# Where a kernel of 17 stages clears its semaphores: in blocks of their own, or inside the next stage

## The chip, the cores and the metric

The kernel runs on one core of a Trainium2 chip. The metric is the device time of one execution in microseconds (us); it is given as the median of several runs. A profiled execution of the same program gives the trace that the rows below are taken from. Of the core's engines, TensorE (PE) multiplies matrices, VectorE (DVE), ScalarE (ACT) and GpSimd (POOL) do the elementwise work, and SyncE (SP) has no arithmetic: it issues transfers and handles semaphores.

## The reference

Two decoder layers over a sequence of 1024 tokens of width 1024, in float32.

```python
for i in range(DEPTH):                      # DEPTH = 2
    a = _rms_norm(h, norm_mix[i])
    h = h + (_even_mixer(a, ...) if i % 2 == 0 else _odd_mixer(a, ...))
    h = h + _hier_moe(_rms_norm(h, norm_ffn[i]), ...)
    h = h + _per_layer_embedding(h, p[i], ...)
```

The even mixer is causal attention with 8 forgetting heads and 8 latent heads; the odd one is a diagonal state-space layer (S5) beside a gated DeltaNet in chunks. The mixture of experts sends each token to 2 of 32 experts (a group first, then two of its eight). The per-layer embedding is a sigmoid gate times a small projection. None of this is touched by the change.

## The kernel before, in words

The program is a straight row of 17 stages; nothing of one stage runs beside another. In order, with the number of semaphores each uses: the constants (2), the even layer's projections (51), its attention (23), the end of the mixer with output projection and routing (37), the experts' first blocks (20), the overflow blocks (12), the layer embedding (26); then for the odd layer the norm (12), a joint stage of S5 columns and powers (14), the S5 chunks (18), a joint stage of the S5 gate, masks, gates and DeltaNet inputs (29), the DeltaNet's preparation (40) and scan (13), the end of the mixer (37), first blocks (20), overflow blocks (12) and the layer embedding (26). Together 392.

A stage is one `nc.Block()`: a region in which every engine gets its own instruction stream, and at whose end all five engines meet at a barrier. [...] Inside a block the engines are tied by semaphores that count up from zero, for transfers (16 each) and for instructions (1 each). The counts in the waits are constants of the stage, so a semaphore must be zero again before its number is given to another stage.

The helper `stage` (line 83) allocates a stage's semaphores, opens the block (line 93) and, when that is closed, calls `clear` (lines 74 to 79 and 95). `clear` opens a second block (line 75) in which SyncE alone has instructions: one `sem_clear` per semaphore (line 79). The other four engines go straight to that block's barrier. Only behind it does the next stage begin. `joint_stage` (line 56) does the same for several helpers that share a block (line 58); their semaphores are gathered in `joint.sems` and cleared at line 61.

```python
def clear(nc, sems):
    with nc.Block() as clearing:
        @clearing.sync
        def _(sp):
            for s in sems:
                sp.sem_clear(s)
```

In the trace the barrier that closes a stage stands under line 93 (15 stages) or 58 (2 joint stages), and the barrier of the clearing block under line 75.

What SyncE does in the stages that matter here: in `overflow_blocks` (line 1530) every engine loads a count of blocks that did not fit and goes through a loop only if it is above zero; with these inputs it is zero. In `layer_embedding` (line 1874) SyncE issues six loads, then for each of 8 token tiles waits until the tile is added and issues its store (line 1919), and at the end waits until all 8 stores have landed. In the norm in front of the odd layer (`rmsnorm_transpose`, line 136) it issues two loads and waits for the second. In the experts' first blocks (line 1623) it issues the weights' loads into a ring of eight places (line 1674). At the start of attention (line 266) TensorE turns queries and keys through one bank (line 362), which ACT and DVE empty in turn. The end of the mixer begins with the output projection on TensorE (line 1243).

Of the kernel before, what the change touches and what calls it, by code (L numbers as in the profile page):

```python
# [30 lines left out]
NUMBER = itertools.count()  # L31


class Steps:
# [3 lines left out]
    def __init__(self, eng, sem, base=0):  # L38
        self.eng, self.sem, self.base, self.n = eng, sem, base, 0
# [7 lines left out]
class Joint:  # L47

    def __init__(self, block, memory):
        self.block, self.memory, self.sems = block, memory, []


@contextmanager
def joint_stage(nc):
    with ExitStack() as memory:
        with nc.Block() as block:
            joint = Joint(block, memory)
            yield joint  # L60
        clear(nc, joint.sems)


@contextmanager
def scope(joint=None):

    if joint is not None:
        yield joint.memory
    else:
        with ExitStack() as memory:  # L70
            yield memory


def clear(nc, sems):
    with nc.Block() as clearing:  # L75
        @clearing.sync
        def _(sp):
            for s in sems:
                sp.sem_clear(s)


@contextmanager
def stage(nc, *names, joint=None):

    with scope(joint) as ctx:
        sems = [ctx.enter_context(nc.semaphore(f"{n}_{next(NUMBER)}")) for n in names]
        if joint is not None:
            joint.sems += sems  # L90
            yield joint.block, sems
            return
        with nc.Block() as block:
            yield block, sems
        clear(nc, sems)


def sbuf(nc, ctx, name, shape, dt=F32):

    return ctx.enter_context(nc.sbuf_tensor(f"{name}_{next(NUMBER)}", shape, dt))  # L100
# [11 lines left out]
def make_constants(nc, c):  # L112

    with stage(nc, "zeroed", "selected") as (block, (zeroed, selected)):
        @block.gpsimd
        def _(pool):
            pool.memset(c.ident[:], 0.0).then_inc(zeroed, 1)
            pool.memset(c.ones[:], 1.0).then_inc(zeroed, 1)
            pool.memset(c.causal[:], 0.0).then_inc(zeroed, 1)
            pool.wait_ge(zeroed, 3)  # L120
            pool.affine_select(out=c.ident[:], in_=c.ident[:], compare_op=ALU.not_equal, fill=1.0,
                               base=0, pattern=[[-1, P]], channel_multiplier=1).then_inc(selected, 1)

            pool.affine_select(out=c.upto[:], in_=c.ones[:], compare_op=ALU.is_ge, fill=0.0,
                               base=0, pattern=[[1, P]], channel_multiplier=-1).then_inc(selected, 1)
            pool.affine_select(out=c.before[:], in_=c.ones[:], compare_op=ALU.is_gt, fill=0.0,
                               base=0, pattern=[[1, P]], channel_multiplier=-1).then_inc(selected, 1)

            pool.affine_select(out=c.causal[:], in_=c.causal[:], compare_op=ALU.is_ge, fill=NEG,
                               base=0, pattern=[[-1, P]], channel_multiplier=1).then_inc(selected, 1)  # L130
            pool.wait_ge(selected, 4)
            pool.tensor_copy(c.ident16[:], c.ident[:])
            pool.tensor_copy(c.causal16[:], c.causal[:])


def rmsnorm_transpose(nc, c, h, gain, normed, xt, width=D, x_dram=None, loads=(), joint=None, h_ready=None):
# [4 lines left out]
    with scope(joint) as ctx:  # L141
# [4 lines left out]
        rstd = sbuf(nc, ctx, "rstd", [P, NT])  # L146
        turned = [psum(nc, ctx, f"turned{a}", [P, 2 * SLAB]) for a in range(2)]
        with stage(nc, "h0_in", "h1_in", "gain_in", "loaded", "squares", "means", "roots", "scaled", "turns", "copied_even",
                   "copied_odd", "vec_steps", joint=joint) as (block, (h0_in, h1_in, gain_in, loaded, squares, means, roots, scaled, turns,
                                                          copied_even, copied_odd, vs)):  # L150
# [115 lines left out]
def attention(nc, c, both, heads, pt, dv, loads):  # L266
# [21 lines left out]
    with ExitStack() as ctx:  # L288
# [10 lines left out]
        turn_high = psum(nc, ctx, "turn_high", [P, SLAB])  # L299
        po = psum(nc, ctx, "po", [2 * dv, SLAB])  # L300
        with stage(nc, "qk_turned", "qk_act", "qk_dve", "scored", "maxed", "exped", "low0_turned", "low1_turned",
                   "high0_turned", "high1_turned", "low0_out", "low1_out", "high0_out", "high1_out", "mixed", "mixed_out",
                   "inverse_turned", "inverted", "inverse_spread", "stored", "loaded", "zeroed", "zeros_out") as (
# [788 lines left out]
def constants(nc, ctx):  # L1092
    c = Constants()
    c.ident, c.ones, c.upto, c.before, c.causal = [
        sbuf(nc, ctx, n, [P, P]) for n in ("ident", "ones", "upto", "before", "causal")]

    c.ident16, c.causal16 = [sbuf(nc, ctx, n, [P, P], BF16) for n in ("ident16", "causal16")]


    c.slots_in = nc.dram_tensor("slots_in", (EXPERTS * REGION + P, D), F32).ap()  # L1100
    c.slots_out = nc.dram_tensor("slots_out", ((2 * EXPERTS + NT) * P, D), F32).ap()
    c.scattered = ctx.enter_context(nc.semaphore("scattered"))
    c.rows_in = [ctx.enter_context(nc.semaphore(f"rows_in{n}")) for n in range(4)]
    c.x_in = [ctx.enter_context(nc.semaphore(f"x_in{n}")) for n in range(2)]
    c.y_out = [ctx.enter_context(nc.semaphore(f"y_out{n}")) for n in range(2)]
    c.h_kept = nc.dram_tensor("h_kept", (S, D), F32).ap()
    make_constants(nc, c)
    return c
# [741 lines left out]
def routing(nc, ctx):  # L1850
    r = Routing()
    r.weights = sbuf(nc, ctx, "weights", [P, 2, NT])
    r.slots, r.results = [sbuf(nc, ctx, n, [P, 2, NT], I32) for n in ("slots", "results")]
    r.table = sbuf(nc, ctx, "table", [1, 5, EXPERTS + 1], I32)
    return r
# [1267 lines left out]
def odd_mixer(nc, c, t, h, layer, r):  # L3123
# [4 lines left out]
    with ExitStack() as ctx:  # L3128
# [9 lines left out]
        with ExitStack() as sub:  # L3138
            q = s5_tiles(nc, sub, h)
            bpow = sbuf(nc, sub, "bpow", [P, 2, PAIRS, P])  # L3140
            with joint_stage(nc) as joint:
                products, evacuate = s5_columns(nc, c, xt, w_in, gbz, u, early, slab_place(h[:, 0:4]), joint)
                s5_powers(nc, c, t, j, q, bpow, joint, products, evacuate)
            s5_chunks(nc, c, t, j, q, bpow, u, scratch=s5_t)
# [5 lines left out]
        with ExitStack() as heads:  # L3150
# [6 lines left out]
            with ExitStack() as prepare:  # L3157
                k = Masks()
                gdn_mask_places(nc, k, prepare)
                with joint_stage(nc) as joint:  # L3160
                    gdn_masks(nc, c, k, joint)
                    sig = sbuf(nc, joint.memory, "sig", [P, 2, SLAB])
                    s5_glu(nc, c, t, j, output_of(u), work[:, 8:12], sig, s5_t, joint)
                    load_rows(nc, [(gains[:], t["gdn_o_norm"][j])], joint)
                    sums, sums_out = gdn_gates(nc, c, t, j, gbz, g, joint)
                    delta_inputs(nc, c, xt, w_in[:, OD_QKV:OD_G], t["gdn_conv_w"][j], [slab_place(work[:, 0:4]), slab_place(work[:, 4:8])],
                                 sig[:].rearrange("p a n -> p (a n)").rearrange("p (t d) -> p t d", t=NT), qkv, sums, sums_out, joint)
                gdn_prepare(nc, c, g, k, qkv, wt, qt, intra_t, scratch)
# [24 lines left out]
def trunk(nc, t, out):  # L3193


    with ExitStack() as ctx:
        c = constants(nc, ctx)
        h = sbuf(nc, ctx, "h", [P, NT, D])
        r = routing(nc, ctx)
        even_mixer(nc, c, t, h, 0, r)  # L3200
        layer_embedding(nc, c, t, h, 0, r, out_dram=c.h_kept)
        odd_mixer(nc, c, t, h, 1, r)
        layer_embedding(nc, c, t, h, 1, r, out_dram=out[0])


# [16 lines left out]
```

## Time and profile before

| What | us |
|---|---|
| Median of 3 runs | 3204.94 (3203.44 to 3205.21) |
| The profiled execution's own time | 3205.38 |
| Its span, from first to last record | 3203.8 |
| TensorE busy | 2941.1 (92%) |
| VectorE busy | 1127.8 (35%) |
| ScalarE busy | 652.4 (20%) |
| GpSimd busy | 242.8 (8%) |
| Mean granted TensorE clock | 0.949 of full |
| DMA, all queues | 617.24 MB, 193 GB/s over the span |

The span is what the trace covers; 1.6 us of the device time lie around it. Register, branch, semaphore and drain instructions are not counted as busy, so a stretch in which all engines only meet at barriers shows as idle on every one of them. "SPq", "PEldq" and the like are the sequencers' own instructions on that engine. [...]

### The profile page before, as it was taken

The page shows a single profiled execution, that of the slowest core. Times are in us where ns is not written, and L with a number is a line of the kernel's source. Part 1 is how long each engine was busy: PE and PEld are TensorE (multiplying, and loading weights), DVE is VectorE, ACT ScalarE, POOL GpSimd, SP SyncE. Part 2 cuts the span into 40 slices and gives each one's busy share as a digit, 9 for nine tenths or more (in the row PEclk, how much of TensorE's full clock was granted, in tenths as well). Part 3 has the DMA queues.
Part 4 walks back from the last instruction along what each step waited for, and adds up shares of the span by engine and source line. Part 5 has one row for each costly group of instructions (what it writes and reads, how often), then busy time and mean ns, then how long its engine had stood idle before and what let it go on. Part 6 is the DMA issues. An engine that isn't in the chain of part 4 may idle for free. (4 is left out here: it accounts for less than half of the span.)

```text
span 3203.8 us, 32783 instructions
## 1 busy us (share of the span) xinstructions
PE 2941.1 (92%) x12473; PEld 1581.4 (49%) x12474; DVE 1127.8 (35%) x2460; ACT 652.4 (20%) x1258; POOL 242.8 (8%) x352
## 2 busy tenths in 40 slices
PE   7999899999799999979889899877997999999798
PEld 5544555545444444424376644476654444444243
DVE  2584355534300000005273625466463000000052
ACT  3310355521110010103121123322211100101030
POOL 0000000001100000011000000043211000000110
PEclk9999899999799999989988799988997999999899
DMA  4000791031599999963120110000415999999641
GB/s 155 27 27 0 309 373 53 1 114 66 198 421 414 413 403 401 400 237 155 44 66 1 15 67 27 0 2 2 167 66 190 422 413 411 410 404 397 233 162 40
DMA packets 138550, 617.24 MB, mean 193 GB/s; under 512 B 25188, under 2 KB 31748, under 8 KB 121992
## 3 DMA queue, kind: packets, MB, share of 16 engines
q1 hardware_dynamic: 110952, 525.93, 41.6%
q0 software_dynamic: 24064, 86.00, 7.0%
q10 hardware_dynamic: 3376, 3.19, 0.3%
q8 instruction: 101, 1.65, 0.2%
q14 instruction: 57, 0.47, 0.0%
HBM read 508.00 MB, written 105.91 MB: 192 GB/s over the span
## 5 line engine op out<-in xcount | busy, mean ns | idle before, releaser
L1974 PE MATMUL acc<-wg,xt 128*128 128x512 f32 x512 | 223.1, 599 | 0.0
L2570 PE MATMUL acc<-xt,work 128*128 128x512 f32 x384 | 166.9, 593 | 0.0
L737 PE MATMUL acc<-h,xt 128*128 128x512 f32 x384 | 165.2, 592 | 0.0
L1974 PEld LDWEIGHTS acc<-wg,xt 128*128 128x128 f32 x512 | 98.5, 193 | 123.4 <-issue 123.4
L376 PE MATMUL scores<-qkt 65*128 65x512 f32 (+7 forms) x384 | 148.9, 498 | 0.9 <-DVE qkt L516 0.9
L522 DVE TENSOR_REDUCE nmax<-scores 128x1 f32<-128x256 f32 (+7 forms) x128 | 96.8, 756 | 77.6 <-PE scores L378 74.5
L1720 PE MATMUL py<-place 128*64 128x512 f32 (+1 forms) x352 | 120.2, 594 | 1.0 <-DVE place L1800 1.0
L1720 PE MATMUL pu<-place 128*128 128x512 f32 (+1 forms) x320 | 119.8, 593 | 0.0
L737 PEld LDWEIGHTS acc<-h,xt 128*128 128x128 f32 x384 | 72.9, 190 | 91.1 <-issue 90.9
L1243 PE MATMUL acc<-place 128*128 128x512 f32 x256 | 114.2, 601 | 2.7 <-PEq L75 2.7
L2570 PEld LDWEIGHTS acc<-xt,work 128*128 128x128 f32 x384 | 72.0, 190 | 86.1 <-issue 86.1
L1806 DVE COPY work<-py 128x512 f32<-128x512 f32 x25 | 17.3, 691 | 242.8 <-PE py L1720 242.8
L1806 DVE COPY place<-py 128x512 f32<-128x512 f32 x25 | 17.3, 691 | 241.1 <-PE py L1720 241.1
L1720 PE MATMUL pg<-place 128*128 128x512 f32 (+1 forms) x288 | 101.6, 596 | 0.0
L469 ACT ACTIVATE probs<-scores,nmax 128x256 f32<-128x256 f32 (+7 forms) x128 | 94.3, 736 | 9.0 <-DVE nmax L522 7.6
L833 ACT ACTIVATE place<-acc 128x256 f32<-128x256 f32 (+4 forms) x88 | 39.8, 473 | 243.3 <-PE acc L737 243.2
L2247 PE MATMUL acc<-s_t,xt 128*128 128x260 f32 (+1 forms) x256 | 86.5, 501 | 2.5 <-PEq L75 2.5
L1839 DVE TENSOR_TENSOR place<-place,pu 128x512 f32<-128x512 f32 x25 | 17.2, 688 | 187.3 <-PE pu L1720 187.3
L1839 DVE TENSOR_TENSOR work<-work,pu 128x512 f32<-128x512 f32 x25 | 17.2, 687 | 186.2 <-PE pu L1720 186.2
L1787 ACT ACTIVATE place<-pg 128x512 f32<-128x512 f32 x25 | 14.9, 597 | 329.1 <-PE pg L1720 329.1
L1787 ACT ACTIVATE work<-pg 128x512 f32<-128x512 f32 x25 | 14.9, 597 | 328.0 <-PE pg L1720 328.0
L376 PEld LDWEIGHTS scores<-qkt 65*128 65x128 f32 (+1 forms) x384 | 64.2, 194 | 33.8 <-issue 33.4
(638 smaller groups left out, 5181.0 us busy)
## 6 DMA issues: line engine op xcount, KB each, us to landing
own<-in_moe_w_gate_dram SPq DMA_DIRECT2D x22, 2048.0 KB, 16.1
place<-in_moe_w_down_dram SPq DMA_DIRECT2D x22, 2048.0 KB, 15.8
place<-in_moe_w_up_dram SPq DMA_DIRECT2D x20, 2048.0 KB, 17.4
slots_out<-zeros SPq DMA_DIRECT2D x4, 9216.0 KB, 62.6
place<-in_moe_w_gate_dram SPq DMA_DIRECT2D x18, 2048.0 KB, 20.5
own<-in_moe_w_up_dram SPq DMA_DIRECT2D x16, 2048.0 KB, 15.4
own<-in_moe_w_down_dram SPq DMA_DIRECT2D x10, 2048.0 KB, 18.9
xt<-in_moe_w_gate_dram SPq DMA_DIRECT2D x9, 2048.0 KB, 22.2
```

The lines of the kernel that those rows point to most:

```text
L376: pe.matmul(bank(n, u)[:, a * SLAB:a * SLAB + w], qkt[0:kind(p).rows, p % 2, u, 0, i * P:(i + 1) * P], qkt[0:kind(p).rows, p % 2, u, 1, a ...
L469: act.activation(probs[:, u, n % 2, 0:(i + 1) * P], bank(n, u), ACT.Exp, bias=nmax[:, n % 2, u:u + 1], accum_out=total[:, (n // NT) % 2, i ...
L522: dve.tensor_reduce(nmax[:, n % 2, u:u + 1], bank(n, u), AX.X, ALU.max, negate=True).then_inc(maxed, 1)
L737: last = pe.matmul(acc[:, n % 4, 0:width], xs[:, k, tile_of(i)], weights[:, k, cols], start=(k == 0), stop=(k == k_of - 1))
L833: last = act.activation(place, part, ACT.Copy)
L1243: last = pe.matmul(acc[:, n, :], columns(k, i), slabs[n][:, k, :], start=(k == 0), stop=(k == KD - 1))
L1720: last = pe.matmul(out[part], lhs[:, k, part], weights_of(kind, q)[:, k, cols], start=(k == 0), stop=(k == k_last), skip_group_check=True)
L1806: dve.tensor_copy(y[:, n % 2, SLAB:D], py[:, SLAB:D]).then_inc(y_dve, 1)
L1839: dve.tensor_tensor(hid, gate, pu[:], ALU.mult).then_inc(hidden, 1)
L1974: last = pe.matmul(acc[:, u % 4, :], xt[:, k, i * P:(i + 1) * P], wg[:, k, n * SLAB:(n + 1) * SLAB], start=(k == 0), stop=(k == KD - 1))
L2247: ins = pe.matmul(acc[:, n % 4, 0:width], xt[:, k, at], slab[:, k, 0:width], start=(k == 0), stop=(k == KD - 1))
L2570: last = pe.matmul(acc[:, n % 4, :], slabs[m // 4 % 2][:, k, (m % 4) * P:(m % 4 + 1) * P], xt[:, k, half * SLAB:(half + 1) * SLAB], start= ...
```

## The change

The clears of a stage move into the next stage's block. A block is now opened by `one_block`, which gives SyncE one more body behind all it has in this block; that body clears the semaphores of the stage before (`Used.sems`). The semaphores stay allocated until then: `Used.held` is closed when the next block is. After the last stage `clear_last` clears that stage's semaphores in a block of its own, as before. The stages' own instructions are the same.

```diff
@@ -47,18 +47,50 @@
 class Joint:
-    def __init__(self, block, memory):
-        self.block, self.memory, self.sems = block, memory, []
+    def __init__(self, block, memory, held):
+        self.block, self.memory, self.held, self.sems = block, memory, held, []
+
+class Used:
+    sems, held = [], None
+
+@contextmanager
+def one_block(nc, held, sems):
+    with nc.Block() as block:
+        yield block
+        if Used.sems:
+            @block.sync
+            def _(sp):
+                for s in Used.sems:
+                    sp.sem_clear(s)
+    if Used.held is not None:
+        Used.held.close()
+    Used.sems, Used.held = sems, held
+
+def clear_last(nc):
+    with nc.Block() as clearing:
+        @clearing.sync
+        def _(sp):
+            for s in Used.sems:
+                sp.sem_clear(s)
+    Used.held.close()
+    Used.sems, Used.held = [], None
 
 @contextmanager
 def joint_stage(nc):
+    held, sems = ExitStack(), []
     with ExitStack() as memory:
-        with nc.Block() as block:
-            joint = Joint(block, memory)
+        with one_block(nc, held, sems) as block:
+            joint = Joint(block, memory, held)
+            joint.sems = sems
             yield joint
-        clear(nc, joint.sems)
@@ -71,28 +103,16 @@
-def clear(nc, sems):
-    with nc.Block() as clearing:
-        @clearing.sync
-        def _(sp):
-            for s in sems:
-                sp.sem_clear(s)
 
 @contextmanager
 def stage(nc, *names, joint=None):
-    with scope(joint) as ctx:
-        sems = [ctx.enter_context(nc.semaphore(f"{n}_{next(NUMBER)}")) for n in names]
-        if joint is not None:
-            joint.sems += sems
-            yield joint.block, sems
-            return
-        with nc.Block() as block:
-            yield block, sems
-        clear(nc, sems)
+    held = ExitStack() if joint is None else joint.held
+    sems = [held.enter_context(nc.semaphore(f"{n}_{next(NUMBER)}")) for n in names]
+    if joint is not None:
+        joint.sems += sems
+        yield joint.block, sems
+        return
+    with one_block(nc, held, sems) as block:
+        yield block, sems
@@ -3201,6 +3221,7 @@
         layer_embedding(nc, c, t, h, 1, r, out_dram=out[0])
+        clear_last(nc)
```

## Rows read from the trace of the kernel before

**Rows 1.** The page, busy us (share of the span) and instructions of TensorE.
```profile
PE 2941.1 (92%) x12473; PEld 1581.4 (49%) x12474; DVE 1127.8 (35%) x2460; ACT 652.4 (20%) x1258; POOL 242.8 (8%) x352
```

**Rows 2.** Windows, one per clearing block: start:end us, busy us per engine, PEclk, DMA, GB/s.
```profile
3.55:3.92 0.37, 0.00 (x0) 0.00 (x0) 0.00 (x0) 0.00 (x0) 0.00 (x0) 1.00 0.00 0
333.96:337.72 3.76, 0.00 (x0) 0.00 (x0) 0.00 (x0) 0.00 (x0) 0.00 (x0) 0.75 0.00 0
682.66:684.22 1.56, 0.00 (x0) 0.00 (x0) 0.00 (x0) 0.00 (x0) 0.00 (x0) 0.92 0.00 0
...
3030.75:3031.67 0.92, 0.00 (x0) 0.00 (x0) 0.00 (x0) 0.00 (x0) 0.00 (x0) 0.50 0.09 18
sum 25.76, PE 0.00 PEld 0.00 DVE 0.00 ACT 0.00 POOL 0.00; mean PE 0.00 PEld 0.00 DVE 0.00 ACT 0.00 POOL 0.00
```

**Rows 3.** Line 79: whole span; windows 333:338, 1590:1599.5, 2240.8:2241.3. ns min/median/max, first to last start us.
```profile
L79 SPq EVENT_SEMAPHORE_RANGE_CLEAR  x392: 25/30/49, 3.7 to 3203.5; - x196
...
L79 SPq EVENT_SEMAPHORE_RANGE_CLEAR  x51: 25/30/38, 334.1 to 337.0; - x51
...
L79 SPq EVENT_SEMAPHORE_RANGE_CLEAR  x26: 25/28/30, 1597.8 to 1599.2; - x26
...
L79 SPq EVENT_SEMAPHORE_RANGE_CLEAR  x2: 31/31/31, 2240.8 to 2241.3; - x2
```

**Rows 4.** Waits of SyncE's queue: waited for, us in total, times, longest.
```profile
SPq L93 <- PEq L93: 876.6, 15, 163.2
...
SPq L58 <- PEq L58: 235.2, 2, 127.1
```

**Rows 5.** Line 93, window 1599.4:1622.95, the norm in front of the odd layer.
```profile
L93 SPq DRAIN  x1: 7/7/7, 1607.2 to 1607.2; - x1
...
L93 DVEq DRAIN  x1: 1258/1258/1258, 1621.5 to 1621.5; - x1
```

**Rows 6.** Line 93, window 1425:1427.4, the first overflow block.
```profile
L93 SPq DRAIN  x1: 7/7/7, 1426.6 to 1426.6; - x1
...
L93 PEldq DRAIN  x1: 72/72/72, 1427.2 to 1427.2; - x1
```

**Rows 7.** Line 93, window 3027:3031.7, the second overflow block.
```profile
L93 SPq DRAIN  x1: 7/7/7, 3030.2 to 3030.2; - x1
...
L93 PEldq DRAIN  x1: 71/71/71, 3030.6 to 3030.6; - x1
```

**Rows 8.** Line 93, windows 1590:1599.5 and 3201:3204, the ends of the layer embeddings.
```profile
L93 DVEq DRAIN  x1: 725/725/725, 1594.1 to 1594.1; - x1
...
L93 SPq DRAIN  x1: 7/7/7, 1597.6 to 1597.6; - x1
...
L93 SPq DRAIN  x1: 7/7/7, 3201.4 to 3201.4; - x1
```

**Rows 9.** Windows around the start of mixer's end, of attention, and in the S5 chunks.
```profile
681.76:684.35 2.59, 0.00 (x0) 0.00 (x1) 0.69 (x1) 0.00 (x0) 0.00 (x0) 0.93 0.00 0
684.40:687.40 3.00, 3.00 (x4) 1.45 (x5) 2.53 (x69) 0.00 (x0) 0.53 (x5) 0.50 0.57 193
...
333.26:337.85 4.59, 0.00 (x0) 0.00 (x0) 0.00 (x0) 0.55 (x1) 0.01 (x1) 0.78 0.00 0
337.85:352.70 14.85, 8.90 (x32) 5.75 (x33) 2.75 (x4) 3.65 (x5) 0.94 (x1) 0.50 0.89 356
352.70:363.10 10.40, 10.37 (x38) 7.94 (x39) 3.85 (x9) 3.84 (x13) 0.00 (x0) 0.50 1.02 407
...
1742.10:1783.00 40.90, 40.75 (x184) 26.25 (x185) 6.85 (x12) 7.16 (x12) 0.00 (x0) 0.50 0.07 7
```

**Rows 10.** Timeline behind the first clearing block: start us, us, engine, what.
```profile
4.04 0.39 SPq L715 DMA_DIRECT2D h<-in_x_dram  x1
...
4.12 0.07 DVE L978 MEMSET prefix<- 128x8 f32 x1 [4.01 <-PEq L75]
```

**Rows 11.** The page, DMA queues: packets, MB, share of 16 engines.
```profile
q8 instruction: 101, 1.65, 0.2%
```

## The prediction

> **What bounds the kernel now.** I first read the busy shares on the page [rows 1]: TensorE works for 2941.1 of 3203.8 us, so the kernel is a row of stages that TensorE fills, and what is left is at most 8% of the span. The change touches only the seams between stages, so the next view is the windows one, cut at the seams. A seam begins when the barrier that closes a stage's block is released (events of line 93, or 58 for a joint stage) and ends when the barrier of the clearing block (line 75) is released. In [rows 2] each such stretch has zero busy time on all five engines and next to no DMA (0.09 at most); the 16 seams that the change removes last 25.76 us together, from 0.37 to 3.76 us each. The reader is to see the zeros: nothing is hidden there, so whatever a seam gives back, the whole program behind it gets. No transfer spans a seam that could become a wait once the seam is shorter.
>
> Then the clears themselves [rows 3]: 392 of them, all by SyncE, one after another. 51 fit between 334.1 and 337.0, which is 2.9 / 50 = 0.058 us from one to the next; 26 between 1597.8 and 1599.2 give 0.056. I use 0.057. What remains of the shortest seam is 0.37 - 2 x 0.057 = 0.26 us: the barrier alone.
>
> Last, where SyncE stands when a block ends. The waits of SyncE's own queue [rows 4] show it waiting 876.6 us in all at the 15 closing barriers of line 93 and 235.2 us at the two of line 58: in most stages it has long finished.
>
> **What the change removes.** 16 of the 17 clearing blocks (the last one stays, as `clear_last`, with the same 26 clears): 16 x 0.26 = 4.2 us of barriers, 366 x 0.057 = 20.9 us of clears, together 25.1; measured 25.76, because in a few seams SyncE stalls between two clears, as at 2240.8, where the next comes at 2241.3 [rows 3]. The term is the measured one: **-25.8 us**.
>
> **What it moves.** The clears go behind SyncE's own program of the next block, so they cost nothing where SyncE is early by more than their length, and all where it is last. No instruction is queued behind them but the block's drain. Block by block:
> - Twelve of the 16 following blocks have cover from the work of the other engines. The tightest is the norm in front of the odd layer: SyncE drains at 1607.2, DVE's drain of 1258 ns starts at 1621.5 [rows 5], so 26 clears (26 x 0.057 = 1.5 us) have 15 us of room. Cost 0. Were that cover gone, all 366 would cost 20.9 us and only the 4.2 us of barriers would be won (a rival below).
> - The first overflow block has no work (its count is zero), so no engine is long in it. SyncE drains at 1426.6, TensorE last at 1427.2 for 72 ns [rows 6]. 20 clears of the block before take 1.14 us: SyncE is now there at 1426.6 + 1.14 = 1427.8, about **+0.5 us**. The second one: 3030.2 + 1.14 = 3031.3 against 3030.6 + 0.07 [rows 7]: **+0.7 us**.
> - The layer embeddings, twice. SyncE is last there: it sends the output and waits for its landing, and drains at 1597.6 when DVE has been done since 1594.1 + 0.7, and at 3201.4 in the second [rows 8]. The 12 clears of the overflow block come behind that wait: 12 x 0.057 = 0.7 each, **+1.4 us**.
> - Semaphores are held one stage longer, so numbers differ; the sum of neighbouring stages is small (51 + 23 the largest), nothing is issued for that. Cost 0.
>
> **The clock of TensorE.** At 682 the clock is full until the seam, TensorE then sits for 2.59 us without work, and the next 3.00 us run at 0.50 with TensorE busy throughout (four matmuls of 512 columns) [rows 9]. The seam itself is 1.56 us, so the idle stretch shrinks to 1.0 us. Half of 3.0 us, **-1.5 us**, would come back if the shorter gap keeps the clock; if not, 0. I take the gain, since work at full density stands on both sides. At the start of attention the clock is low for 25 us after a gap of 4.59 us [rows 9], but the work there is thin (TensorE busy 8.90 of 14.85 us): I take 0 and keep the bound for a rival.
>
> **Costs that no row shows.** With the seam goes the time in which the engines' sequencers could fetch what comes next. Bounds: below 0, by the seam of 0.37 us, after which SyncE and DVE start the next stage's first instructions at 4.04 and 4.12, 0.12 and 0.20 us behind the release at 3.92 [rows 10]. That start needs no more than a barrier's worth of idle time. Above, one stall of the size seen among the clears (0.5 less the pace, 0.43 us) at each of 16 seams, 6.9 us. I take 0, by the nearer row, and keep 6.9 for the range.
>
> [...]
>
> **Sum** against the profiled execution (span 3203.8, time 3205.4, so 1.6 lies around the span): 3203.8 - 25.8 + 0.5 + 0.7 + 1.4 - 1.5 = 3179.1; plus 1.6 = 3180.7. The median of the three runs, 3204.94, is 0.4 below the profiled one, so **3180.3 us**, 0.77% less.
>
> **Rivals.**
> - *The clock stays up through the seams.* Attention's head would run at full speed: TensorE's busy time from 337.85 to 363.1 is 8.90 + 10.37 = 19.3 us at 0.50 [rows 9], so at most 9.6 us more are won: 3180.3 - 9.6 = 3170.7. For it: the 4.59 us gap falls to 0.8. Against: from 1742.1 on, TensorE is busy 40.75 of 40.90 us and stays at 0.50 [rows 9]; narrow matmuls and transposes are slow there for ten times as long as any gap lasts. Chance 0.12. [...]
> - *Exposed fetches, partly.* The page counts 101 packets of the queue q8 "instruction" with 0.2% of 16 engines' span [rows 11]: 0.002 x 3203.8 x 16 / 101 = about 1.0 us each. Anything from 0.43 to 1.0 us at each seam costs 6.9 to 16 us: 3187 to 3196, still faster. Chance 0.12.
> - *SyncE is late everywhere*, or the barriers stay: the clears move without cover and only barriers are won: 3204.9 - 4.2 = 3200.7, within 0.2%. Against it stand the 1112 us that SyncE waits [rows 4]. Chance 0.04.
> - *Slower: fetches on the path at each seam.* [...] Price: more than one packet of 1.0 us in sequence per seam. The net gain of 23.2 us is used up at 23.2 / 16 = 1.45 us per seam, and it is slower by 0.2% beyond 1.85; two packets each give 3204.9 - 23.2 + 32 = 3213.7. Rows 10 speak against it. Chance 0.02.
>
> **How the numbers follow.** Forecast as summed 0.70, clock rival 0.12, partly exposed fetches 0.12, no gain 0.04, slower 0.02. A measurement of this kernel tells about 0.2% (6.4 us) from no change. The first three are all faster by more: 0.94; within 0.2%: 0.04; slower: 0.02. Range: low 3171, the clock rival in full; high 3189, the forecast with 6.9 us of stalls and without the clock's 1.5. What falls outside is part of the fetch rival and the last two, some 0.15.
>
> **What would show it.** In the profile after, right: one clearing block instead of 17, at the end, still some 2.2 us; 16 barriers fewer; the first instruction of each stage 0.1 to 0.2 us behind the release of the block before; 392 clears in all, 366 of them while other engines are busy; SyncE last at the barrier in both overflow blocks and in both layer embeddings, with the 12 clears between its last wait and its drain; full clock from the first matmul behind attention. Each stage's own length otherwise the same: a stage that grew by over 1 us at its start speaks for the fetch rival, one that shrank by some us for the clock. The forecast is wrong if SyncE's drain comes last in a block not named here, or if the time is not between 3171 and 3189.

## The result, and the profile after

The changed kernel takes **3159.26 us** (median of four runs: 3159.78, 3158.57, 3158.73, 3178.30) against 3204.63 for the kernel before on the same chip: ratio 0.9873, 95% interval 0.9836 to 0.991. The forecast was 3180.3 with a range of 3171 to 3189. The sign was right, but the gain is 45.4 us where 24.6 were forecast, and the time lies below the range. The profiled execution took 3159.78 us over a span of 3158.2, against 3205.38 and 3203.8 before: 45.6 us less.

The page of the changed kernel, busy us per engine, beside [rows 1]:

```profile
PE 2916.5 (92%) x12473; PEld 1569.3 (50%) x12474; DVE 1128.2 (36%) x2460; ACT 652.6 (21%) x1258; POOL 243.5 (8%) x352
```

This is the first sign of what happened. The same 12473 matmuls are busy 24.6 us less, while the busy times of VectorE, ScalarE and GpSimd stand within 0.7 us of where they were. The 16 seams that went have 0.00 us of busy time on every engine [rows 2], so their removal does not explain this. A higher granted clock does: its mean went from 0.949 to 0.959, and 18.9 of the 24.6 us lie in one stage, the S5 chunks, where TensorE's busy time for the same 544 matmuls fell from 97.94 to 79.06 us while the granted clock rose from 0.70 to 0.86 (windows below).

The parts that the prediction named, first. Lines of clears, SyncE's waits and SyncE's drains in the changed kernel (70 is the line of the clears in the next block, 81 that of the last block, 64 the barrier that closes a stage). The windows are the whole span for the first three, then the closing of the first overflow block, of the second, and of the last layer embedding:

```profile
L70 SPq EVENT_SEMAPHORE_RANGE_CLEAR  x366: 25/30/39, 222.8 to 3156.2; - x183
L81 SPq EVENT_SEMAPHORE_RANGE_CLEAR  x26: 25/28/30, 3156.5 to 3157.9; - x26
...
SPq L64 <- PEq L64: 1089.1, 17, 164.3
...
L70 SPq EVENT_SEMAPHORE_RANGE_CLEAR  x20: 25/30/31, 1410.6 to 1411.7; - x20
...
L64 PEldq DRAIN  x1: 71/71/71, 1410.8 to 1410.8; - x1
...
L64 SPq DRAIN  x1: 7/7/7, 1411.8 to 1411.8; - x1
...
L64 PEldq DRAIN  x1: 69/69/69, 2984.2 to 2984.2; - x1
...
L64 SPq DRAIN  x1: 7/7/7, 2985.4 to 2985.4; - x1
...
L64 SPq DRAIN  x1: 7/7/7, 3156.3 to 3156.3; - x1
```

All 366 clears are there, and SyncE still waits 1089.1 us at the 17 closing barriers. In both overflow blocks its drain now comes about 1 us behind TensorE's, as its 20 clears lie there. The last block is still there, with 26 clears.

The start of the second stage, behind the release at 3.55, in the timeline of the changed kernel:

```profile
3.67 0.39 SPq L735 DMA_DIRECT2D h<-in_x_dram  x1
...
3.74 0.07 DVE L998 MEMSET prefix<- 128x8 f32 x1 [3.63 <-PEq L64]
```

0.12 and 0.19 us behind the release, as in [rows 10]. In each of the 16 stages some engine has its first instruction 0.10 to 0.13 us behind the release: no delay at a stage's start speaks for the rival of exposed fetches.

Now each stage's own length, from the release of one closing barrier to the next. The release is told by GpSimd's second semaphore event at the barrier. At the first clearing block of the kernel before that event is at 3.9 us, behind the drains of all five engines (3.6 to 3.8) and ahead of one event on each of the other four (4.0):

```profile
L75 POOLq EVENT_SEMAPHORE  x2: 17/17/17, 3.8 to 3.9; - x2
L75 POOLq DRAIN  x1: 41/41/41, 3.6 to 3.6; - x1
...
L75 SPq DRAIN  x1: 7/7/7, 3.8 to 3.8; - x1
L75 SPq EVENT_SEMAPHORE  x1: 17/17/17, 4.0 to 4.0; - x1
```

The lengths:

| Stretch | Before | After | Difference |
|---|---|---|---|
| 16 seams | 25.76 | none | -25.8 |
| projections | 330.03 | 329.47 | -0.6 |
| attention | 344.94 | 340.08 | **-4.9** |
| end of the even mixer | 163.06 | 161.60 | -1.5 |
| first overflow block | 1.67 | 2.58 | +0.9 |
| first layer embedding | 169.38 | 171.11 | +1.7 |
| S5 columns and powers (joint) | 116.95 | 118.37 | +1.4 |
| S5 chunks | 111.57 | 92.94 | **-18.6** |
| DeltaNet's preparation | 163.31 | 166.03 | +2.7 |
| scan | 34.97 | 33.66 | -1.3 |
| end of the odd mixer, first blocks | 746.26 | 744.64 | -1.6 |
| second overflow block | 1.46 | 2.58 | +1.1 |
| second layer embedding | 169.88 | 170.91 | +1.0 |
| last clearing block | 2.18 | 1.71 | -0.5 |

The other four stretches differ by 0.2 us in sum. The seams gave what was forecast. One stage that the prediction took to stay as it was gave 18.6 us more. Windows of the S5 chunks, in the kernel before (the first 30 us, then the stage; the figure behind the five engines is PEclk, the granted clock as a share of full):

```profile
1741.81:1771.81 30.00, 29.84 (x132) 18.73 (x133) 4.91 (x11) 4.18 (x7) 0.00 (x0) 0.51 0.01 1
1741.81:1853.37 111.56, 97.94 (x544) 71.26 (x544) 57.69 (x94) 15.39 (x25) 0.00 (x0) 0.70 0.10 11
```

and in the changed one (the first 30 us, the stage, then the stage cut where the clock changes):

```profile
1724.94:1754.94 30.00, 27.56 (x256) 21.49 (x256) 13.36 (x25) 10.30 (x17) 0.00 (x0) 1.00 0.22 23
1724.94:1817.88 92.94, 79.06 (x544) 61.51 (x544) 57.71 (x94) 15.18 (x25) 0.00 (x0) 0.86 0.13 14
...
1725.10:1757.80 32.70, 27.56 (x256) 21.46 (x256) 16.19 (x29) 10.40 (x17) 0.00 (x0) 1.00 0.27 29
1757.80:1764.60 6.80, 3.63 (x33) 3.33 (x33) 6.65 (x13) 0.00 (x0) 0.00 (x0) 0.50 0.39 41
1764.60:1798.70 34.10, 30.92 (x202) 23.77 (x200) 30.98 (x49) 3.58 (x6) 0.00 (x0) 1.00 0.00 1
```

The stage has 544 matmuls in both. Before, it runs its first 132 in 30 us at a clock of 0.51. After, it runs 256 in 30 us at 1.00, and TensorE even has gaps (27.56 of 30 us busy). The stretch of [rows 9] that was low for 41 us is gone. What stays low is what was low before as well: 6.8 us at 1757.8 (then at 1793.3), in a wait of TensorE for VectorE (TensorE busy 3.63 us of them, VectorE 6.65), and the last 19 us of the stage, the third line below. TensorE's idle time ahead of the stage's first matmul fell from 1.97 us to 0.94: the seam of 1.03 us was all that went. Here are that first matmul before and after, and that last stretch:

```profile
1741.97 0.96 PE L2343 MATMUL pa<-ident,bpow 128*128 128x128 f32 x4 [1.97 <-PEq L75]
...
1725.10 0.63 PE L2363 MATMUL pa<-ident,bpow 128*128 128x128 f32 x4 [0.94 <-PEq L64]
...
1798.82:1817.88 19.06, 16.96 (x56) 12.92 (x56) 3.77 (x6) 1.20 (x2) 0.00 (x0) 0.50 0.00 0
```

The gap does not leave the clock low at once. Before the change, too, the stage begins at full clock, and the clock falls 0.3 us in:

```profile
1741.81:1742.11 0.30, 0.14 (x2) 0.17 (x3) 0.11 (x4) 0.00 (x0) 0.00 (x0) 1.00 0.00 0
1742.11:1771.81 29.70, 29.70 (x132) 18.56 (x132) 4.80 (x9) 4.18 (x7) 0.00 (x0) 0.50 0.01 1
```

The two seams that the prediction looked at for their clock, in the changed kernel: the gap ahead of the mixer's end and the first matmuls behind it, then the gap ahead of attention and the stretches behind it:

```profile
672.37:673.24 0.87, 0.00 (x0) 0.02 (x1) 0.56 (x1) 0.00 (x0) 0.00 (x0) 1.00 0.00 0
673.30:676.30 3.00, 3.00 (x7) 1.36 (x8) 2.54 (x70) 0.00 (x0) 0.53 (x5) 1.00 0.59 188
...
332.30:333.20 0.90, 0.02 (x1) 0.05 (x1) 0.00 (x0) 0.57 (x1) 0.06 (x1) 1.00 0.00 0
333.17:341.20 8.03, 3.88 (x24) 2.44 (x24) 1.87 (x3) 1.78 (x3) 0.92 (x1) 1.00 0.78 314
341.20:351.50 10.30, 8.50 (x32) 6.55 (x33) 3.19 (x8) 4.40 (x12) 0.00 (x0) 0.50 1.02 408
```

At the mixer's end the clock stays at 1.00: seven matmuls start in the 3.00 us that held four in [rows 9]. Attention starts at 1.00 as well and falls 8 us in, for 10.2 us instead of 27.3.

### The profile page after: what moved, and what is told of

It reads as the page before. It is cut to its first block and busy times, and to the rows that moved or that the text cites. A ratio compares the mean times of both kernels' runs of the same rounds, so it can differ in the third digit from the quotient of the medians.

```text
span 3158.2 us, 32607 instructions
## 1 busy us (share of the span) xinstructions
PE 2916.5 (92%) x12473; PEld 1569.3 (50%) x12474; DVE 1128.2 (36%) x2460; ACT 652.6 (21%) x1258; POOL 243.5 (8%) x352
## 5 line engine op out<-in xcount | busy, mean ns | idle before, releaser
L1807 ACT ACTIVATE place<-pg 128x512 f32<-128x512 f32 x25 | 14.9, 597 | 329.0 <-PE pg L1740 329.0
L1807 ACT ACTIVATE work<-pg 128x512 f32<-128x512 f32 x25 | 14.9, 597 | 328.9 <-PE pg L1740 328.9
## 6 DMA issues: line engine op xcount, KB each, us to landing
place<-in_moe_w_up_dram SPq DMA_DIRECT2D x20, 2048.0 KB, 17.8
```

## Experiments

Two theories for the 18.6 us of the S5 chunks. **Gap**: the 1.97 us without work for TensorE ahead of this stage bring the clock down at the stage's start, and the stage's first work does not bring it back. **Place**: something else in the changed kernel (a later or earlier start, other semaphore numbers, the clears beside the work) decides. Most kernels below are the changed one with a switch: a clearing block stays behind chosen stages, with all of its clears, with none, or with small matmuls for TensorE. In all of them a stage's semaphores are given free one stage later, as in the changed kernel. "Stage 8" is the joint stage ahead of the S5 chunks, "stage 1" the projections ahead of attention.

```diff
     Used.n += 1
+    if n in KEEP:                       # clears kept in the seam block
+        with nc.Block() as clearing:
+            ... SyncE: the first KEEP[n] clears of stage n
+            ... if n in FILL: TensorE: FILL[n] times
+                pe.matmul(bank, c.ones[:], c.ident[:], ...)
```

**1. Only the S5 seam removed.** `KEEP` = every stage but 8.

> The clearing block behind the joint stage of S5 columns and powers is the only one taken away (its 14 clears move into the S5 chunks); the other 15 stay. [...] Rival 'place': the clock there depends on when the stage comes, moved by the 17 us won ahead of it, not on its own seam; then 3204.6 - 1.0 = 3203.6 us with the chunks at 111.6 us.

By the gap theory this one seam is worth 1.0 + 18.6 us: 3204.6 - 19.6 = 3185.0 us, with the chunks near 93 us.

Measured: 3183.77 us (four runs, 3182.34 to 3187.35), ratio 0.9934 (0.9917 to 0.9951). First 30 us of the chunks, and the stage:

```profile
1742.90:1772.90 30.00, 27.56 (x256) 21.50 (x256) 13.36 (x25) 10.29 (x17) 0.00 (x0) 1.00 0.22 23
1742.90:1834.22 91.32, 77.45 (x544) 60.39 (x544) 57.69 (x94) 15.18 (x25) 0.00 (x0) 0.88 0.13 14
```

One seam of 1.03 us is worth some 20 us. The gap theory stands, and the stage begins at 1742.9, 1.1 us from where it began before: the place in time is not it.

**2. Only the S5 seam kept.** `KEEP` = {8: all}.

> As after the change, but the S5 chunks' own seam (14 clears, 1.0 us) is put back. Gap: the clock is lost there again, 3159.3 + 1.0 + 18.6 = 3178.9 us, chunks near 111.6 us. Place: 3159.3 + 1.0 = 3160.3 us, chunks near 93 us.

Measured: 3176.35 us (3174.91 to 3176.55), ratio 0.9911 (0.9895 to 0.9928).

```profile
1728.68:1758.68 30.00, 29.84 (x136) 19.23 (x137) 4.90 (x11) 4.18 (x7) 0.00 (x0) 0.52 0.01 1
1728.68:1837.01 108.33, 94.72 (x544) 69.53 (x544) 57.69 (x94) 15.29 (x25) 0.00 (x0) 0.73 0.11 12
```

The slow head is back, in the otherwise changed kernel. Here the clock falls a little later, after 1.2 us of the stage; its first microsecond is still full:

```profile
1728.68:1729.68 1.00, 0.84 (x7) 0.67 (x8) 0.15 (x4) 0.17 (x1) 0.00 (x0) 1.00 0.00 0
```

Together, 1 and 2 put the effect in this seam.

**3. The S5 seam kept, TensorE busy in it.** `KEEP` = {8: all}, `FILL` = {8: 3}; the seam lasts 1.20 us.

> As the kernel with only the S5 seam kept, but TensorE runs three small float32 matmuls (12 instructions of 128 columns, some 1.3 us) of constants into a spare bank inside that clearing block; nobody reads them. [...] If the barrier or the SyncE clears themselves cost the clock, as if only the seam were kept: 3179 us. [...]

By either theory the chunks take about 93 us and the whole about 3161 us: by the gap theory because TensorE is not idle in the seam, by the place theory because the seam does not matter.

Measured: 3170.18 us (3172.83, 3155.62, 3169.89, 3170.47), ratio 0.9878 (0.9853 to 0.9903). The last line is a stretch later in the same stage:

```profile
1728.73:1758.73 30.00, 27.57 (x256) 21.52 (x256) 13.36 (x25) 10.28 (x17) 0.00 (x0) 1.00 0.22 23
1728.73:1830.82 102.09, 88.31 (x544) 68.93 (x544) 57.70 (x94) 15.18 (x25) 0.00 (x0) 0.76 0.11 12
1760.60:1791.30 30.70, 24.99 (x123) 20.13 (x123) 21.06 (x37) 1.19 (x2) 0.00 (x0) 0.50 0.11 12
```

The three small matmuls are 6 instructions in the trace, busy 0.91 us, not the 12 and 1.3 us of the estimate. The head is at full clock although the barrier and the clears stand. But here the drop that comes some 32 us into the stage lasts 30.7 us where the changed kernel's lasts 6.8. So there is a second place in this stage where the clock falls, and how long it stays low varies. The profiled span is 11.9 us above the changed kernel's with the seam taken off (3171.3 - 1.2 - 3158.2); 9.2 of them are in this stage (102.09 for 92.94) and 2.2 in attention (342.26 for 340.08). That is why the time lies between 3161 us and the 3179 us expected if the barrier or the clears themselves cost the clock.

**4. The S5 seam kept, but empty** (a barrier, no clears). `KEEP` = {8: 0}; the seam lasts 0.33 us.

> As after the change, with an empty block (a barrier, no clears, 0.26 us) at the S5 seam; its 14 clears are in the chunks. TensorE's idle stretch is 1.1 to 1.2 us, between 0.9 (clock kept) and 1.9 (lost). Gap: if the stretch has to be near 1.9 us to lose the clock, 3159.6 us with the chunks at 93; if 1.2 is already too long, 3178.2 us; runs that differ among themselves by 19 us would say that it stands on the edge. Place: 3159.6 us.

Measured: 3169.1 us, ratio 0.9899 (0.9869 to 0.9929), and the four runs are 3160.40, 3177.81, 3178.20, 3160.00. The profiled one:

```profile
1726.10:1756.10 30.00, 27.56 (x256) 21.50 (x256) 13.37 (x25) 10.29 (x17) 0.00 (x0) 1.00 0.23 23
1726.10:1818.94 92.84, 78.97 (x544) 61.54 (x544) 57.71 (x94) 15.18 (x25) 0.00 (x0) 0.86 0.13 14
```

Two groups of times 18 us apart and nothing between them. The mean granted clock of the runs differs with them: 0.959 and 0.961 in the two shorter, 0.954 and 0.953 in the two longer. With 1.27 us of idle TensorE the same program keeps its clock or loses it. A median over such runs is a count of which outcome came up, not the price of a barrier.

**5. The changed kernel again**, five runs.

> The changed kernel once more, unchanged, for the spread of its times. [...] Rival 'one value': the 3178.3 us was a disturbance; all runs within 3 us of 3159.3.

If the chunks keep the clock in most executions and lose it in some, the times fall into two groups, near 3159 and near 3178 us, in the kernel before with the weights turned round.

Measured: 3159.95 us (3158.23 to 3162.54), ratio 0.9878 (0.9855 to 0.9902). With the first four runs, eight of nine lie between 3158 and 3163 and one at 3178.3, at a clock of 0.953. The kernel before has the two groups as well: of the 49 runs made of it in all, 7 lie between 3186 and 3191 (clock 0.953 to 0.955) and 42 between 3202 and 3209 (0.947 to 0.951).

**6. The exposed clears covered.** Neither overflow block clears anything: its predecessor's semaphores are carried on, and the layer embedding's SyncE clears all 32 behind its six loads, before it waits for the first tile.

```diff
+CARRY = (5, 15)                          # the overflow blocks
+                clear_now(sp)            # layer_embedding, behind the six loads
                 for i in range(NT):
                     sp.wait_ge(added, 2 * i + 2)
```

> As after the change, but no clear is exposed: the overflow blocks clear nothing (their stage before's semaphores are carried on), and the layer embeddings clear all 32 behind their six loads, ahead of the wait for the first store. Both theories of the exposed clears say: each overflow block 2.58 to 1.67 and 1.46 us, each embedding 0.7 us shorter, 0.9 + 1.1 + 0.7 + 0.7 = 3.4 us, so 3155.9 us where the chunks keep the clock (3174.9 where they don't). If the embeddings' other 1.0 us of growth was the clock, it stays or goes by chance. If the clears among running transfers cost something, no gain.

Measured: 3159.05 us (3152.28 to 3159.98), ratio 0.9873 (0.985 to 0.9896). The clears in the first layer embedding (its line 65), then the windows of the first overflow block and of that embedding, and those of the changed kernel:

```profile
L65 SPq EVENT_SEMAPHORE_RANGE_CLEAR  x32: 2/25/273, 1436.1 to 1438.5; - x32
...
1409.31:1410.99 1.68, 0.00 (x0) 0.00 (x0) 0.00 (x0) 0.00 (x0) 0.00 (x0) 0.50 0.02 5
1410.99:1582.17 171.18, 152.62 (x400) 72.59 (x400) 67.97 (x92) 36.65 (x66) 18.21 (x16) 0.94 0.30 117
```

```profile
1409.29:1411.87 2.58, 0.00 (x0) 0.00 (x0) 0.00 (x0) 0.00 (x0) 0.00 (x0) 0.50 0.05 13
1411.87:1582.98 171.11, 153.32 (x400) 72.86 (x400) 68.03 (x92) 36.88 (x66) 18.93 (x16) 0.93 0.30 117
```

The overflow blocks are back at 1.68 and 1.48 us, so their clears had cost 0.90 and 1.10. From the last store to the end of the first embedding it is 2.88 us again instead of 3.62, so the clears there had cost 0.74. Yet the embedding is no shorter. Its part ahead of the last store took 0.8 us more than in the changed kernel (171.18 - 171.11 + 0.74). The clock is not the reason: it was low for less of the embedding (mean 0.94 for 0.93). TensorE waited longer for the projection's weights, here and in the changed kernel:

```profile
1422.75 2.47 PE L1990 MATMUL acc<-wp,pt 128*128 128x512 f32 x3 [2.40 <-DMA wp<-in_ple_w_proj_dram]
...
1422.55 3.78 PE L1977 MATMUL acc<-wp,pt 128*128 128x512 f32 x4 [0.82 <-DMA wp<-in_ple_w_proj_dram]
```

In the second embedding it is 2.62 us for 0.50. The clears come 24 us behind the issue of that load, so they are not what delayed it; SyncE's issue of it took 1.43 us for 0.58 in the first embedding and 1.68 for 0.63 in the second, and why is open. By medians the 3.4 us expected came to 0.9; this profiled execution (span 3150.7) is the shortest of the five.

**7. As 6, with three small matmuls behind the last product of the joint stage** ahead of the S5 chunks, into a spare bank, so that TensorE works up to the barrier and idles for 0.30 us ahead of the chunks.

```diff
+                if last == 3 * NT:
+                    for k in range(3):
+                        pe.matmul(spare[:], c.ones[:], c.ident[:], ...)
```

> As clears_covered, and TensorE goes on with three small float32 matmuls of constants into a spare bank behind its last product of the joint stage, while ScalarE empties the last bank, so it is idle for 0.3 instead of 0.9 us ahead of the S5 chunks. Gap: every execution keeps the clock at the start of the chunks; 3155.9 us and no second heap at +18. Rival (the loss inside the chunks, 33 us behind their start, is what varies): times still spread over up to 18 us.

Measured: 3154.73 us (3150.56 to 3158.94), ratio 0.9857 (0.9833 to 0.9882); on the same chip 5.2 us under run 5. It has the lowest median of all versions. All five runs are in the shorter group, though so were eight of nine without the tail: five runs don't show that it makes the clock safe.

**8. The attention seam kept.** `KEEP` = {1: all}; the seam lasts 3.16 us.

> As after the change, but the seam ahead of attention (51 clears, 3.8 us) is put back. Gap: attention is back at its length of before, 344.9 instead of 340.1 us, so 3159.3 + 3.8 + 4.8 = 3167.9 us where the S5 chunks keep the clock (3186.5 where they don't). Place: 3163.1 us.

Measured: 3167.47 us (3165.89 to 3167.71), ratio 0.9899 (0.9872 to 0.9927). Attention, first 25 us and whole, here, then in the changed kernel:

```profile
335.92:360.92 25.00, 18.90 (x80) 13.36 (x81) 7.46 (x15) 8.44 (x21) 0.95 (x1) 0.59 0.94 376
335.92:678.84 342.92, 315.87 (x1792) 196.11 (x1792) 182.74 (x304) 173.05 (x401) 0.95 (x1) 0.97 0.43 172
```

```profile
333.02:358.02 25.00, 18.91 (x94) 13.35 (x95) 9.73 (x18) 10.36 (x26) 0.95 (x1) 0.80 0.94 376
333.02:673.09 340.07, 313.00 (x1792) 194.08 (x1792) 182.74 (x304) 173.25 (x401) 0.95 (x1) 0.98 0.44 174
```

Attention gives back 2.8 us of its 4.9; with the seam's 3.2 that is 6.0 of the 6.1 us between the two profiled spans (3164.3 and 3158.2). The median rose by 7.5 over run 5; the other 1.4 us have no place in this profile. The 2.8 us are not all the seam's: in the profiles of runs 2 and 3, which have no seam here, attention takes 342.24 and 342.26 us, with the clock falling 4.4 us in. Attention's length without a seam thus varies from 340.1 to 342.3, and one profile of each kernel does not show how much of the 4.9 us is the gap's.

**9. All seams there, TensorE busy in 15 of them** (4 to 15 small matmuls each). The seams then last 43.6 us together, 17.8 more than before.

> All 16 clearing blocks are kept as before the change, but behind 15 of them (all but the first) TensorE multiplies constants (4 to 15 small float32 matmuls, about as long as the clears take) into a bank nobody reads any more. No seam is removed, so no part of the 25.8 us is won; exposed clears (3.4 us) are not paid either. Gap: the clock's share of the gain comes alone: attention -4.9, end of the mixer -1.5, S5 chunks up to -18.6 (some executions -9, as with only that seam filled): 3203 - 6.4 - 9 to 18.6 = 3178 to 3188 us. Rival 'it is the removed time that counts, the clock follows the place': 3203 us.

Measured: 3189.51 us (seven runs, 3185.9 to 3199.18), ratio 0.9961 (0.9942 to 0.9979). The S5 chunks, and attention's first 25 us:

```profile
1742.05:1833.38 91.33, 77.45 (x544) 60.38 (x544) 57.72 (x94) 15.18 (x25) 0.00 (x0) 0.88 0.13 14
...
336.95:361.95 25.00, 18.89 (x84) 13.26 (x85) 8.37 (x16) 9.24 (x23) 0.95 (x1) 0.66 0.94 375
```

Its profiled span is 3185.9: 3203.8 + 17.8 of longer seams leaves 35.7 us that the stages gave, with no barrier and no clear removed. That is what the clock can give where TensorE works through 15 of the seams; in the changed kernel the stages gave 45.6 - 25.8 = 19.8 us. It comes from the S5 chunks (-20.2), the experts' first blocks (571.3 each, -3.4 and -4.1), attention (-3.0) and smaller ones. The first blocks were not expected to give anything.

**10. The attention seam kept, TensorE busy in it.** `KEEP` = {1: all}, `FILL` = {1: 15}; the seam lasts 3.88 us.

> As attention_seam_kept (3167.5 us, attention 342.9 us in its profile), with TensorE busy with 15 small matmuls in that seam. [...]

By the gap theory attention is back near 340.1 us and the whole at 3159.5 + 3.8 = 3163.3 us; if idling is not the reason, it stays at 3167.5.

Measured: 3165.89 us (3164.91 to 3167.21), ratio 0.9886 (0.9863 to 0.991); attention 342.23 us, hardly less than the 342.92 of run 8. **Not what was expected**: the clock falls at 340.5, 4 us into attention, whatever went before it, for 17.1 us. With the gap closed or filled, attention still loses the clock within 4 to 8 us. Its head is thin work (TensorE busy 3.88 of 8.03 us in the changed kernel's window above), which may be the reason; no run made it denser. What a gap changes is how soon the clock falls: in run 8 after 1.2 us of attention, in the kernel before already in the seam.

**11. All seams there, all empty.** `KEEP` = every stage with 0 clears; each lasts 0.33 us.

> As after the change, with an empty block (barrier, no clears) at each of the 16 seams. Gap: only 0.3 us more without work at each seam, 3159.5 + 16 x 0.3 = 3164.3 us where the S5 chunks keep the clock, some 3182 where they do not, and both heaps seen, as with the empty block at that seam alone (3160.0 and 3160.4, 3177.8 and 3178.2). If the barriers carried more of the 25.8 us than 0.26 each, it is slower than this by the difference.

Measured: 3180.16 us (3182.04, 3180.64, 3179.68, 3164.47), ratio 0.9914 (0.9885 to 0.9943); the profiled one:

```profile
1729.28:1759.28 30.00, 29.84 (x140) 19.20 (x140) 4.90 (x11) 4.18 (x7) 0.00 (x0) 0.54 0.01 1
1729.28:1839.39 110.11, 96.48 (x544) 71.16 (x544) 57.71 (x94) 15.39 (x25) 0.00 (x0) 0.71 0.11 11
```

16 barriers of 0.33 us are 5.3 us, and the short run stands just that above the changed kernel's. The other three, one of them the profiled run, stand 15 to 18 us higher. In the profiled one the first 2.00 us of the chunks still run at 1.00, then the clock falls. The barrier itself took 0.33 us, and here three runs of four were 15 to 18 us longer: it adds 0.33 us to a gap of 0.94.

**12. All seams there, TensorE busy in the S5 seam alone.** Every clearing block stands with all of its clears, as in the kernel before; four small matmuls are in the block behind stage 8. Besides them only one thing differs from the kernel before: semaphores are given free one stage later, as in runs 1 to 4.

```diff
+KEEP = {0: None, 1: None, ... 15: None}   # None: all clears of that stage
+FILL = {8: 4}
```

> All 16 clearing blocks as before the change; the one edit is 4 small float32 matmuls of constants on TensorE in the block ahead of the S5 chunks (into a bank nobody reads any more). In the kernel with all seams filled that seam took 1.43 us instead of 1.03. [...] Place: 3204.7 us, with 3187 as seldom as in the kernel before (4 of 33).

By the gap theory the chunks start at full clock in every execution: 3204.3 + 0.4 - 18.6 = 3186.1 us where they keep it to the end, some 3195 where they lose it 33 us in, and none near 3204.

Measured: 3187.55 us (11 runs, 3185.38 to 3193.16), ratio 0.9959 (0.9944 to 0.9975) against 3202.98 for the kernel before beside it.

```profile
1740.57:1770.57 30.00, 27.56 (x256) 21.48 (x256) 13.38 (x25) 10.29 (x17) 0.00 (x0) 1.00 0.22 23
1740.57:1833.99 93.42, 79.55 (x544) 61.89 (x544) 57.69 (x94) 15.18 (x25) 0.00 (x0) 0.85 0.13 13
...
1739.31 1.13 PE L93 MATMUL pc<-ident,ones 128*128 128x128 f32 x8 [0.94 <-PEq L68]
...
1740.73 0.63 PE L2389 MATMUL pa<-ident,bpow 128*128 128x128 f32 x4 [0.30 <-PEq L83]
```

The last two lines are the small matmuls and the first one of the chunks: TensorE's idle time of 1.97 us is cut into 0.94 and 0.30.

The seam became longer (1.43 us for 1.03), the kernel does more work, and it is 15.4 us faster by medians. All eleven runs are under 3194, where only 7 of 49 of the unedited kernel are. Each other stage is within 1 us of its length in the kernel before. Later release of the semaphores is not the reason, since run 2 has it and the slow head as well. This settles the cause: it is TensorE's idling at this seam.

The outcomes at the S5 seam side by side; the group of each run is told by its time and granted clock, and only one run of each kernel has a trace. Run 3 is left out, since its second drop hides the first outcome in the times:

| TensorE at the S5 seam | Idle ahead of the chunks | Clock kept, runs |
|---|---|---|
| idle, barrier and clears (kernel before; run 2) | 1.97 us | 7 of 49; 0 of 4 |
| idle, barrier alone (runs 4, 11) | 1.27 us | 2 of 4; 1 of 4 |
| no seam (changed kernel; runs 1, 6, 8, 10) | 0.94 us | 8 of 9; 17 of 17 |
| working in the seam (runs 9, 12) | 0.94 us, then 0.30 | 6 of 7, one unclear (3199.18); 10 of 11, one unclear (3193.16) |
| no seam, working up to the barrier (run 7) | 0.30 us | 5 of 5 |

## Why the prediction was wrong, step by step

**The seams, -25.8: right.** They are gone to the hundredth, since nothing was hidden in them and nothing filled them.

**Hidden clears at 0, held semaphores at 0: right.** All stages but those named have SyncE waiting at the end as before.

**The overflow blocks, +0.5 and +0.7: right in place, too small.** Measured +0.9 and +1.1, and run 6 takes them back in full. The 20 clears take the 1.1 us that they were priced at (1410.6 to 1411.7). But they were priced as starting where SyncE's drain had stood, 0.9 us into the stage (1426.6 - 1425.7), and they start 1.3 us in (1410.6 - 1409.3). Why SyncE comes to them 0.4 us later is not shown.

**The embeddings' ends, +0.7 each: right.** From the last store to the end it is 3.62 us for 2.88, and 3.65 for 2.90. The stages grew by 1.7 and 1.0 in all. The remaining 1.0 and 0.3 lie ahead of the first store. TensorE's clock fits them: it comes back up 14.8 us into the first embedding for 10.0 before, and 14.7 for 14.3 in the second. No run was made for it.

**No exposed fetch, 0: right.** First instructions come 0.12 to 0.19 us behind the release in either kernel. That anything is fetched while the engines idle in a seam was an assumption; no run shows it. The trace gives no cause for the stall of 0.43 us between two clears either, so that it was a fetch, as the fetch rival's price took it, is not shown.

**The clock at the mixer's end, -1.5: right**, 1.46 us. Run 9 bears it out: with its seam longer but filled, that stage takes 161.69 us for 163.06.

**The clock elsewhere, 0: the step that failed.** The words were that from 1742.1 on "narrow matmuls and transposes are slow there for ten times as long as any gap lasts", and they served as the reason against the rival of a clock that stays up. The row [rows 9] (40.75 of 40.90 us busy at 0.50) was read as what that work does to the clock. It was the outcome of the gap ahead of it: the same matmuls run at 1.00 for their first 30 us where the idle time ahead is 0.94 us or is filled (runs 1, 3 and 12). Half right was that this work does not bring the clock back: it stayed low for 41 us with TensorE busy throughout. The row had the warning in it. By the halving that the prediction used for attention, this work at full clock needs about half of 40.75 us, so a bound of 20 us belonged into the range beside attention's 9.6; 18.6 were measured. The two seams that I did examine were chosen for their low clock behind them, and at this third one the low clock was put down to the stage.

**The rival "the clock stays up": right in kind, wrong in its places.** It had attention's head alone, at -9.6, and a chance of 0.12. Attention gave half of that in the profiled run, where its head still loses the clock 8 us in; the S5 chunks gave twice it. The gap that decided was short: 1.97 us ahead of the chunks against 0.94.

The sum with what was measured: 3203.8 - 25.8 (seams) - 18.6 (chunks) - 4.9 (attention) - 1.5 (mixer's end) + 2.0 (overflow) + 2.8 (embeddings) + 4.1 (columns, preparation) - 3.8 (all others) = 3158.1, against a span of 3158.2. The 4.1 us of the columns and the preparation go with a clock that falls at another moment than before: in the columns 7.8 us in, behind a wait of TensorE of 3.05 us (before, low from the start for 5.6 us, with a wait of 0.61), and in the preparation for 46.8 us in all instead of 40.6. No run was made for them, so their cause is not shown.

## What to carry to other kernels

Price an idle stretch of TensorE twice: by its own length, and by the low clock behind it, which here lasted 41 us although TensorE was busy all the time; take half of the busy time at 0.50 behind each gap as the bound (20 us for the chunks, where 18.6 were won; 9.6 for attention, where 4.9 were). A row of work at low clock does not say whether the work or the gap ahead of it is the cause, so look whether the same kind of work runs at full clock elsewhere, or put a few small matmuls in the gap. When runs fall into two groups, count the groups before comparing medians.

## What the runs showed of the hardware that was not expected

- A stage with two outcomes: in the profiles the same S5 chunks take 91 to 93 us, or 108 to 112 us where the clock falls at their start (and 102 once, in run 3, by the later drop). By the times, it fell in 5 of 8 runs with a gap of 1.27 us and in 46 of 53 with 1.97.
- The clock does not fall in that gap but behind it, with TensorE at work again: 0.3, 1.2 and 2.4 us into the stage in the kernel before and runs 2 and 11. It then stays low for 40.9, 37.1 and 37.6 us, with TensorE busy in all but 0.15 us of it.
- An empty block at a seam took 0.33 us (runs 4 and 11), and runs with it at the S5 seam came out 15 to 18 us longer in 5 of 8 cases.
- With TensorE busy through the seams (run 9) the experts' first blocks were 3.4 and 4.1 us shorter: their clock is low for 8.8 us instead of 14.9, and for 8.4 instead of 15.6.
